# The first four levels of a triangular inverse as 16x16 substitutions on GpSimd, in a recurrence of nine tiles

## The reference, cut to what matters

```python
def step(S, inp):
    r_t, w_t, k_t, v_t, kk_t, a_t = inp
    sa = jnp.einsum("bhvk,bhk->bhv", S, -kk_t)
    S = (S * w_t[:, :, None, :] + sa[..., None] * (kk_t * a_t)[:, :, None, :]
         + v_t[..., None] * k_t[:, :, None, :])
    return S, jnp.einsum("bhvk,bhk->bhv", S, r_t)
```

## Time and profile before

| | |
|---|---|
| median of three runs | 1555.64 us |
| the profiled execution | 1553.69 us |
| its span, first to last instruction | 1552.0 us |
| mean granted clock of PE | 0.961 |
| PE busy | 1437.4 us, 93% of the span |
| DVE, ACT, POOL busy | 522.6, 369.2, 197.8 us |
| L1317 products (TI by LTm, XX by TT, TT by XX) | 52.8 + 58.8 + 59.9 us busy, x3936 |

### The profile page before, as it was taken

One profiled execution on the slowest core, in us unless ns is written; L12 is line 12 of the kernel. 1 busy time (PEld: TensorE's weight loads), 2 busy tenths in 40 slices (PEclk: granted clock), 3 DMA queues, 4 the chain that ended last, 5 costly groups with the idle time before them and its releaser, 6 DMA issues. The chain is left out here.

```text
span 1552.0 us, 28560 instructions
## 1 busy us (share of the span) xinstructions
PE 1437.4 (93%) x12027; PEld 1040.5 (67%) x12027; DVE 522.6 (34%) x986; ACT 369.2 (24%) x765; POOL 197.8 (13%) x323
## 2 busy tenths in 40 slices
PE   5899999999996999999999999966999999999965
PEld 3566666566664877777777786735877878788832
DVE  4245644720201444444444454345000010000027
ACT  5332232401202323223233332220011111111132
POOL 4002212200002202012012011011000000000043
PEclk9999999999997999999999999976999999999987
DMA  9337656622141371312412302027879997988457
GB/s 351 102 97 242 229 149 227 233 71 84 57 129 51 100 235 45 110 40 72 110 34 79 110 14 64 1 61 271 314 256 374 384 390 287 325 327 326 164 209 266
DMA packets 168473, 271.19 MB, mean 175 GB/s; under 512 B 18760, under 2 KB 89030, under 8 KB 168344
## 3 DMA queue, kind: packets, MB, share of 16 engines
q1 hardware_dynamic: 153480, 221.65, 42.6%
q0 software_dynamic: 12560, 39.29, 6.7%
q10 hardware_dynamic: 2304, 8.39, 1.3%
HBM read 214.70 MB, written 54.59 MB: 174 GB/s over the span
## 5 line engine op out<-in xcount | busy, mean ns | idle before, releaser
L2294 PEld LDWEIGHTS banks<-moe_xT,moe_wg 128*128 128x128 f32 x1024 | 131.3, 191 | 8.9 <-issue 7.8
L2294 PE MATMUL banks<-moe_xT,moe_wg 128*128 128x128 f32 (+4 forms) x1024 | 135.4, 291 | 0.8 <-DVE moe_xT L2617 0.8
L2294 PE MATMUL banks<-moe_xT,moe_wu 128*128 128x128 f32 (+4 forms) x1024 | 134.5, 290 | 0.5 <-DMA moe_wu<-w_expert_up 0.5
L2294 PEld LDWEIGHTS banks<-moe_xT,moe_wu 128*128 128x128 f32 x1024 | 131.2, 191 | 0.7 <-DMA moe_wu<-w_expert_up 0.7
L1653 POOL TENSOR_TENSOR mixer_LTm<-mixer_LT,level 128x256 f32<-128x256 f32 (+1 forms) x90 | 71.9, 822 | 405.3 <-ACT mixer_LTo L1721 281.2
L664 PE MATMUL banks<-xT,w_v 128*128 128x352 f32 (+1 forms) x384 | 118.6, 469 | 1.8 <-ACT sig_w L808 1.8
L664 PE MATMUL banks<-xT,w_r 128*128 128x352 f32 (+1 forms) x384 | 118.6, 469 | 0.0
L664 PE MATMUL banks<-xT,w_k 128*128 128x352 f32 (+1 forms) x384 | 118.3, 468 | 0.0
L1349 PE MATMUL banks<-mixer_w_out,mixer_yT 128*128 128x512 f32 x256 | 117.6, 617 | 0.0
L2323 PE MATMUL banks<-moe_wd,moe_hid 128*128 128x512 f32 x256 | 112.5, 593 | 0.0
L664 PEld LDWEIGHTS banks<-xT,w_v 128*128 128x128 f32 x384 | 72.8, 190 | 45.6 <-issue 2.8
(11 more groups left out here) (489 smaller groups left out, 1944.2 us busy)
## 6 DMA issues: line engine op xcount, KB each, us to landing
...
moe_wu<-w_expert_up SPq DMA_DIRECT2D x16, 2048.0 KB, 12.7
moe_wd<-w_expert_down SPq DMA_DIRECT2D x16, 2048.0 KB, 11.2
...
```

The costliest lines, as they stand in the source:

```text
L2294: mm = pe.matmul(bank[:, i * n:(i + 1) * n], wt[:, p % 2, q, (t0 + i) * P:(t0 + i + 1) * P], xT[:, p % 2, q, 0:n], start=q == 0, stop=q == ...
```

## The change

Levels 0 to 3 are gone from PE, ACT and DVE. In their place each 16x16 diagonal block is inverted by substitution on POOL: 30 tensor_tensor operations over 64 partitions, each waiting for the one before (`substitution`). One partition holds one 16x16 block of one head. To get there the data go through DRAM: ACT copies the diagonal scores to LT and stores them (`scores_of_half`), SP loads the 16x16 diagonals (`load_diagonals`), and after POOL SP stores the inverses and loads them as `blocks` (`store_inverse`, `load_blocks`). DVE spreads them to block form in TX, which holds TT and TI, and transposes them in squares of 32 (`spread`). Levels 4 and 5 and the last pair remain.

The order on the engines is new. The scores of tile n+1 are made in the middle of tile n; level 4's product of tile n+1 stands at the end of tile n behind Y; tile n's quarter-pieces of `wo` stand between the masked scores. The load of features is split: rows 0 to 19 and 28 to 35 first, the gates' rows 20 to 27 and 36 to 39 later. The loops have the same trips. The blocks of tiles 0 and 1 are inverted in the projection: PE makes their diagonal scores in eight calls of `diagonal`, and POOL runs the substitution over 128 partitions there. First loads of weights and rows no longer wait for the inverse's levels.

PE, the start of tile 1 in the program before: from the level 2 product (TI by LTm) to level 3's first products. L1292 are transposes, L1331 and L1336 the sums for norms.

```diff
+DIAG = 16 * 64 + 16
...
+def scores_of_half(d, u, h):
+    return d["scores"][u].rearrange("(j h) e -> h j e", h=2)[h, :, 0:4096].rearrange("j (p c) -> p j c", c=64)
...
+def diagonals(d, u):
+    return d["scores"][u].rearrange("m (b e) -> (m b) e", b=4)[:, 0:1024].rearrange("b (r c) -> b r c", c=64)[:, :, 0:16]
...
+def substitution(pool, U, N, V, part, strict, ident, m, then, last):
+    G_ = pool
+    then(G_.tensor_tensor(N[0:m], U[0:m], strict[0:m], ALU.mult))
+    then(G_.tensor_tensor(V[0:m], N[0:m], ident[0:m], ALU.add))
+    for r in range(14, 0, -1):
+        shape = [m, r, 15 - r]
+        to = part[0:m, 0:r * (15 - r)].rearrange("p (s t) -> p s t", s=r)
+        rows = V[0:m, 0:r, r + 1:16]
+        then(G_.tensor_tensor(to, N[0:m, 0:r, r:r + 1].to_broadcast(shape), V[0:m, r:r + 1, r + 1:16].to_broadcast(shape), ALU.mult))
+        add = G_.tensor_tensor(rows, rows, to, ALU.add)
+        (last if r == 1 else then)(add)
...
+            pool.wait_ge(sg("first_scores_out"), 64)
+            for u in range(2):
+                pool.dma_start(U16[64 * u:64 * u + 64, :, :], diagonals(d, u)).then_inc(sg("first_U16_loaded"), 16)
...
+            pool.wait_ge(sg("first_U16_loaded"), 32)
+            substitution(nc.gpsimd, U16, N16, V16, part16, c["strict16"], c["ident16"], P, then, then)
+            for u in range(2):
+                pool.dma_start(d["inverse"][u], V16[64 * u:64 * u + 64, :, :].rearrange("p s t -> p (s t)")).then_inc(sg("first_V16_out"), 16)
...
+            def diagonal(j, g):
+                need(pe, sg("diagonal_read"), j)
+                need(pe, sg("diagonal_done"), 2 * j + g)
+                pe.wait_ge(sg("made_A"), j + 1)
+                pe.wait_ge(sg("made_B"), j + 1)
+                q = slice(64 * g, 64 * g + 64)
+                for u in range(2):
+                    for v in range(2):
+                        at = slice(P * u + 64 * v, P * u + 64 * v + 64)
+                        mm = pe.matmul(banks[64 * v:64 * v + 64, 7 * 512 + 64 * (2 * u + g):7 * 512 + 64 * (2 * u + g) + 64],
+                                       out["B"][q, at], out["A"][q, at], start=True, stop=True)
+                mm.then_inc(sg("diagonal_done"), 1)
...
-            def load_feats(n, u, m):
-                before = reg(sp, n - 1)
-                for name in ("O_done", "Y_done", "yg_made", "yr_made"):
-                    w(sp, name, before)
-                cols = bass.ds(n * P, m)
-                for lo, hi in ((0, 16), (16, 28), (28, 40)) if n else ((F_EARLY, F_TILES),):
+            def load_feats(n, m):
+                u, cols = n % 2, bass.ds(n * P, m)
+                w(sp, "O_done", n - 1)
+                w(sp, "Y_done", n - 1)
+                for lo, hi in ((0, 20), (28, 36)):
                     sp.dma_start(feats[u][:, lo:hi, 0:m], feat[:, lo:hi, cols]).then_inc(sg(f"feats{u}_loaded"), 16)
...
+            def load_gates(n, m):
+                u, cols = n % 2, bass.ds(n * P, m)
+                w(sp, "yg_made", n - 1)
+                w(sp, "yr_made", n - 1)
+                for lo, hi in ((20, 28), (36, 40)):
+                    sp.dma_start(feats[u][:, lo:hi, 0:m], feat[:, lo:hi, cols]).then_inc(sg(f"gates{u}_loaded"), 16)
+            def load_diagonals(n):
+                w(sp, "scores_out", 32 * (n - 1) if n < NP else 32 * (NP - 2) + 16)
+                w(sp, "V16_made", n - 2)
+                sp.dma_start(U16[:, :, :], diagonals(d, n % 2)).then_inc(sg("U16_loaded"), 16)
+            def store_inverse(n):
+                w(sp, "V16_made", n - 1)
+                w(sp, f"blocks{n % 2}_loaded", 16 * (n // 2))
+                sp.dma_start(d["inverse"][n % 2], V16[:, :, :].rearrange("p s t -> p (s t)")).then_inc(sg("V16_out"), 16)
+            def load_blocks(n, m):
+                w(sp, "V16_out", 16 * (n - 1))
+                w(sp, "TX_made", 2 * (n - 1))
+                of_tile = d["inverse"][n % 2].rearrange("(j b) (r c) -> (b r) j c", b=8, c=16)
+                sp.dma_start(blocks[0:m, n % 2], of_tile[0:m]).then_inc(sg(f"blocks{n % 2}_loaded"), 16)
...
+            load_blocks(1, P)
+            second_loads()
+            third_loads()
+            for n in range(2, NT):
+                m = P if n < NP else DEC
+                load_feats(n, m)
+                load_diagonals(n)
+                load_gates(n, m)
+                if n == 2:
+                    later_loads()
+                store_inverse(n)
+                load_blocks(n, m)
                 load_x(n - 1)
                 store(n - 2, P)
...
-                    w(pe, "gvar_read", n0)
+                    w(pe, "TGV_read", n + 1)
                     pe.matmul(by_four(psum[7], n0), headones[:, :], yrs[:, :, lanes(n0)], start=True, stop=True).then_inc(sg("var_done"), 1)
-                def wo(half, part):
+                def wo(part, half):
                     def run():
                         if part == 0:
                             if late:
-                                w(pe, ("TI1_made", "TT1_made")[half], back.xx + half)
+                                w(pe, ("TI1_made", "TT1_made")[half], 2 * n + 1 + half)
                             else:
-                                w(pe, ("ATT0_read", "ATT1_read")[half], back.n1)
+                                w(pe, f"TI{1 - half}_made", 2 * n + 2)
                             w(pe, "yr_made", n0)
...
+                if n == 0:
+                    for turned in (tb, tv, tgv, tk, tki, mt, rbt, rkt, att):
+                        turned()
+                    for g in range(2):
+                        product(0, 4, g, P)
+                    level(4)
+                    for g in range(2):
+                        product(0, 5, g, P)
+                    level(5)
+                    diagonal_scores(1, P)
+                else:
+                    tb()
+                    behind("mu")
+                    level(4)
+                    tv()
+                    tgv()
+                    for g in range(2):
+                        product(n, 5, g, m)
+                    behind("var")
+                    tk()
+                    level(5)
+                    tki()
+                    behind("gvar")
+                    if m_next:
+                        diagonal_scores(n + 1, m_next)
+                    mt()
+                    if not last:
+                        behind("wo0a")
+                    rbt()
+                    if not last:
+                        behind("wo1a")
+                    rkt()
+                    if not last:
+                        behind("wo0b")
+                    att()
+                    if not last:
...
+                u_rows()
+                if m == P:
...
                     pe.matmul(y, SA[0:m, 64 * h:64 * h + 64], RBT[0:m, g, i * P:i * P + m], start=False, stop=False)
                     mm = pe.matmul(y, tV[0:m, 64 * h:64 * h + 64], RKT[0:m, g, i * P:i * P + m], start=False, stop=True)
                 mm.then_inc(sg("Y_done"), 1)
+                if m_next:
+                    w(pe, "ht1_read", n0)
+                    for g in range(2):
+                        product(n + 1, 4, g, m_next)
...
+            def invert(n):
+                w(pool, "U16_loaded", 16 * (n - 1))
...
+                substitution(nc.gpsimd, U16, N16, V16, part16, c["strict16"], c["ident16"], 64, then, last)
...
+            def masks(n, m):
+                for k in (4, 5):
                     for g in range(2):
                         w(pool, f"LT{g}_read", 3 * n + (3 if m == P else 1))
-                        w(pool, f"X{g}_done", 6 * n + max(k - 3, 0))
-                        nc.gpsimd.tensor_tensor(LTm[0:m, k % 3, g, :, :], LT[0:m, g, :, :], over4(c["level"][0:m, k, :]), ALU.mult).then_inc(sg(f"LTm{g}_made"), 1)
-            steps(pool, front)
-            front(8, 0, DEC, 8, 9, 10, 0)
+                        w(pool, f"X{g}_done", 3 * n - 3 + k - 3)
+                        nc.gpsimd.tensor_tensor(LTm[0:m, k - 4, g, :, :], LT[0:m, g, :, :], over4(c["level"][0:m, k - 4, :]), ALU.mult).then_inc(sg(f"LTm{g}_made"), 1)
+            for n in range(NT):
+                m = P if n < NP else DEC
+                masks(n, m)
+                if n > 1:
+                    invert(n)
...
+                if n > 1:
+                    w(act, "U16_loaded", 16 * (n - 3))
+                    for g in range(2):
+                        w(act, f"LT{g}_read", 3 * n + m // 64)
+                    for h in range(m // 64):
+                        act.dma_start(scores_of_half(d, n % 2, h), LT[64 * h:64 * h + 64].rearrange("p g i c -> p (g i) c")).then_inc(sg("scores_out"), 16)
+                if m == P:
+                    for g in range(2):
+                        nc.scalar.copy(LTo[:, n % 2, g, :, :], psum[g][0:64, :].rearrange("p (a b) -> p a b", a=4)[:, :, 64:P]).then_inc(sg(f"LT{g}_read"), 1)
...
+                def spread(n, m):
+                    w(dve, f"blocks{n % 2}_loaded", 16 * (n // 2 + 1))
```

(18 more changed lines are left out.)

498 lines of the change are left out of this document (249 added, 249 removed).

## The result

| | before | after |
|---|---|---|
| median of the runs | 1555.64 us (1551.04 to 1558.54) | 1479.4 us (1477.55 to 1484.35) |
| ratio, 95% interval | | 0.952 [0.9485, 0.955] |
| the profiled execution, its span | 1553.69, 1552.0 us | 1477.55, 1475.8 us |
| mean granted clock of PE | 0.961 | 0.950 |
| PE busy | 1437.4 us | 1364.1 us |

The change made the kernel 4.8% faster. The forecast was 1475 us with a range of 1461 to 1510, and faster by more than 0.3% had 0.95.

A forecast was written before the change was run, and what follows sets the result against it. PE was taken to bound each full recurrence tile. Stage terms +2.5 projection, +3 start, -16 first to second, -62 six tiles, -6 tile 8 sum to -78.5 from 1553.69 us: forecast 1475 us, range 1461 to 1510.

The forecast's parts named there:

- A full tile 48.3 us: Full recurrence tile: 58.62 us less 11.0 of PE work and pauses, plus 0.3 wait, 47.9; taken as 48.3.
- The pauses covered by the outputs, 1.2 us: PE's three pauses of about 0.4 us per tile go, covered by output products between the masks: 1.2 us.
- The chain: Next tile's scores through ACT, DRAM, POOL and DVE to the transposed blocks: done at 43.4, needed at 48.3, 4.9 us left.
- Projection +2.5 (0 to 5): Before the first scores: 32 added 64x64 matmuls in 8 places, 0.3 to 0.5 us each, +2.5 us.
- Tile 0, +3: Start to first L1507: 32.7 us before, now 31 plus 4 to 5 for lowered clock; +3 (-2 to +6).
- First to second -16: First to second L1507: 62.6 us before, now 48.3 less 3.0 plus 1.5 for late ACT, 46.6; -16 us.
- Tile 8 -6: Half-size last tile: removed levels and swap 10 us, 2 to 4 returning as pauses; -6 (-9 to -2).
- 1 (the chain late): Before product 4: POOL or the four transfers take longer and PE waits for the blocks; 1503 to 1527 us, chance 0.13.
- 2 (POOL slows DVE's norm): POOL's work overlaps DVE's norm, whose two instructions double, delaying h2's transposes; 1493 to 1516 us, chance 0.12.
- Rival 4: POOL's inverse: 1.0 us per instruction however small, 30 us in all; 1584 us, slower than before; chance 0.04.
- Rival 3: Mid-tile scores: features arrive late for them; with the clock 1490 to 1510 us, chance 0.06.
- Rival 5: Tile 0 keeps its clock and nothing waits: 47.6 us a tile, tile 0 at -2; 1462 us or less, chance 0.08.

The follow-up runs named there:

- the second pair: Kernel before and changed kernel each profiled once more, unedited: 1560.72 us and 1481.12 us; spans 1559.0 and 1473.6 us.
- the added matmuls: Matmuls on the identity with unused results, added round tile 0 where PE waits, against the changed kernel: 1475.12 us, ratio 0.9461 to the kernel before.
- the other set with both kernels: Changed kernel run again, unedited, beside the kernel before on another chip: 1481.12 us, ratio 0.9511; the kernel before's median there 1557.9 us.

## Why the prediction was right, step by step

- **A full tile 48.3 us.** 48.34 measured. The terms stand: a level is 2.8 us of matmuls and, by the sum, some 0.3 round them; product 4 follows Y; h2's wait is 0.38 to 0.54 us where 0.3 was worked out. The last 0.4 is luck: the terms gave 47.9, and I took 48.3 for a slowing of DVE that did not come (its norm kept 1.28 and 1.22 us). Of what came in its place 0.14 us is h2's wait in this tile and about 0.25 lies spread over the rest of it. Two tiles in six take 1.5 to 1.8 us more: in the first of them the clock is 0.58 from 594 to 598 us, 12 us into the tile; such dips come without a pause too. The kernel before has one such tile of 60.19 in six. That is the 1.8 us missing in the six tiles.
- **The pauses covered by the outputs, 1.2 us.** Right for this order, but the cover is worth more than I priced: without it the three pauses are 1.44 us each.
- **The chain.** In t, from product 4 at 650.23: scores' end 12.4 for 12.5, ACT's copies done 14.3 for 14.4 (the terms written give 14.0), the stores landed by 18.8 (SP's next issue) for 17.5, U16 landed 21.5 for 21.1, POOL's end 33.0 for 34.1, blocks 38.2 for 40.3, spread and transpose done 43.8 for 43.4, need 48.35 for 48.3. POOL's 30 instructions took 11.5 us for 13, because a small one costs 0.36 from start to start and not 0.45. The nearest row, a memset's slope and wait, gave 0.28; the foot of the earlier trace rows was too high. The four small transfers landed in 2.6, 2.6, 2.9 and 2.2 to 2.5 us (medians) for 3.1, 2.6, 2.6 and 2.6. My slack was wrong in one place: the blocks were to land at 40.3 and the router's sum to come at 42, so POOL had these 1.7 us on top of the 4.9, and rivals 1 and 4 are priced that much too high in each tile. The slack measured is 8.6 us, about the 4.9, these 1.7, and the 2.1 us by which the blocks land earlier.
- **Features.** The load did not hold the scores in any tile. Its 28 rows, in two DMAs, take 3.06 us to issue.
- **Projection +2.5 (0 to 5): measured +2.4 to +7.8 over all profiles, +6.0 in the first.** This step failed in size. Of the first pair's 6.0 us the calls are 1.2, where I had 2.5; 0.6 lies ahead of the first feature round; what I missed is the pause, 1.6 longer, and behind a pause of 3 us or more the lowered clock, 2.6 us (L753 3.64 us for 1.95, L839 2.97 for 2.10).
- **Tile 0, +3: measured 0.** The clock was as low as feared, 0.50 from 500 to 524 us, but I counted part of it twice: my 2.1 us for the scores was a row at the lower clock already, and the masks (11.7 us for 10.4) and the two levels (8.1 for 8.0) took at that clock nearly what I had given them. All the terms together were 32.6 us for 31, and I added 4 to 5 us on top.
- **First to second -16: measured -12.8, and -17.1 in the second pair**, because the kernel before needs 62.58 or 66.95 us here. In absolute terms I forecast 46.6 (the terms give 46.8) and the changed kernel takes 49.8 us, in two other profiles 54.5. The clock is at 0.50 to 0.65 for 8 to 18 us behind ACT's 2.01 us of lateness, which I had at 1.5 us with no price on the clock; with the added matmuls the clock stays up and the distance is 45.72 us.
- **Tile 8 -6: measured -4.5, and -7.2 in the second pair.** Three waits for DVE's masks, 0.90, 1.04 and 0.89 us, are 2.8 us, inside the 2 to 4 I had for pauses. The changed kernel repeats here to 0.07 us, the kernel before differs by 2.75, so the forecast lies within what its two profiles leave open.
- The misses of +3.5, -3.0, +3.2, +1.8 and +1.5 and the -4.7 behind the recurrence, which I take for chance, sum to +2.3 us. The total is better than its parts: that it came within 0.3% is partly luck. The second pair of profiles has -85.4 us, the medians have -76.2 and, in the other set with both kernels, -76.8.

**The rivals.** 1 (the chain late) did not occur and would have from 8.6 us more of POOL, where the forecast wrote 4.9. 2 (POOL slows DVE's norm) is refuted: with POOL busy all through it, the norm keeps its length. I had read the doubling in the earlier trace rows as a rule for every pair; there L1653 of POOL, 0.8 us long, had started 0.17 us ahead of a DVE instruction of 0.43 us. The Trainium skill, SBUF — State Buffer, section SBUF: two separate sides, says that whichever of the two starts first keeps the shared pair for its whole instruction and the other blocks. By that rule, the traces agree, a DVE instruction of 1.2 us loses at most the 0.3 us left of a small one, and POOL waits it out: 1.19 us for 0.25. Rival 4 (0.86 us an instruction) is far off at 0.36. Rival 3 (features late) did not occur. Rival 5 is what the added matmuls brought in part.
